# A fused two-block network on one core: the rotary embedding's partition-block transfers issued from SyncE's queue instead of ScalarE's

## The reference, cut to what matters

```python
def rope(x):
    half = HEAD_DIM // 2
    ...
    x1 = x[..., :half].astype(jnp.float32)
    x2 = x[..., half:].astype(jnp.float32)
    out = jnp.concatenate([x1 * cos - x2 * sin, x2 * cos + x1 * sin], axis=-1)
    return out.astype(x.dtype)
...
    qa = rope(rms_norm(to_heads(a_q, N_HEADS_MOBA), qk_g[0]))
    ka = rope(rms_norm(to_heads(a_k, N_HEADS_MOBA), qk_g[1]))
```

## Time and profile before

| | |
|---|---|
| median of 3 runs | 2808.93 us (2806.44 to 2811.38) |
| profiled execution | 2807.05 us |
| its span (first to last instruction) | 2805.2 us |
| PE busy | 2519.4 us (90%) |
| DVE busy | 1328.8 us (47%) |
| POOL busy | 1128.6 us (40%) |
| ACT busy | 1075.1 us (38%) |
| DMA issues `raw<-in_stream`, SPq | 206 of 1024 KB |
| DMA issues `hraw<-xs`, ACTq | 96 of 64 KB |

### The profile page before, as it was taken

One profiled execution on the slowest core, in us unless ns is written; L12 is line 12 of the kernel. 1 busy time (PEld: TensorE's weight loads), 2 busy tenths in 40 slices (PEclk: granted clock), 3 DMA queues, 4 the chain that ended last, 5 costly groups with the idle time before them and its releaser, 6 DMA issues.

```text
span 2805.2 us, 31247 instructions
## 1 busy us (share of the span) xinstructions
PE 2519.4 (90%) x11290; PEld 2022.4 (72%) x11290; DVE 1328.8 (47%) x2101; ACT 1075.1 (38%) x1530; POOL 1128.6 (40%) x828
## 2 busy tenths in 40 slices
PE   6999999679999999999997799999988687896867
PEld 5887887457887888887875578878866565765656
DVE  5454034654444034440255544540676666566663
ACT  4333233534332143331334443331454442464542
POOL 3554445214455445554453044544532222422222
PEclk9999999789999999999998799999999898998989
DMA  3222223102222222222232022222321211211111
GB/s 146 99 91 104 90 104 106 60 16 90 101 93 90 93 102 91 91 103 90 104 105 75 1 90 105 90 105 90 135 68 46 68 46 46 99 52 67 47 66 60
DMA packets 37470, 233.25 MB, mean 83 GB/s; under 512 B 5632, under 2 KB 5632, under 8 KB 10624
## 3 DMA queue, kind: packets, MB, share of 16 engines
q1 hardware_dynamic: 30816, 218.12, 21.8%
q10 hardware_dynamic: 6560, 13.84, 1.7%
HBM read 223.55 MB, written 2.10 MB: 80 GB/s over the span
## 4 chain that ended last, share of the span: by engine, by line
issue 62%; POOL 37%; POOLq 1%
POOL w_lo L412 37%; POOLq L406 0%; POOLq L410 0%; POOLq L202 0%; POOLq L412 0%; POOLq L1776 0%
## 5 line engine op out<-in xcount | busy, mean ns | idle before, releaser
L412 POOL TENSOR_TENSOR w_lo<-raw,w_hi 128x512 fp32r<-128x512 f32 x824 | 1128.4, 1401 | 1676.0 <-ACT w_hi L854 1675.7
L420 PE MATMUL ps<-h_hi,w_hi 128*128 128x512 f32 x2304 | 928.3, 403 | 32.3 <-DVE h_lo L1234 10.7
L421 PE MATMUL ps<-h_lo,w_hi 128*128 128x512 f32 x2304 | 907.7, 394 | 0.0
L422 PE MATMUL ps<-h_hi,w_lo 128*128 128x512 f32 x2304 | 906.2, 393 | 0.0
L854 ACT ACTIVATE w_hi<-raw 128x1024 fp32r<-128x1024 f32 x412 | 413.2, 1051 | 841.2 <-PE ps L422 833.1
L420 PEld LDWEIGHTS ps<-h_hi,w_hi 128*128 128x128 f32 x2304 | 439.8, 191 | 132.7 <-issue 18.8
L421 PEld LDWEIGHTS ps<-h_lo,w_hi 128*128 128x128 f32 x2304 | 439.8, 191 | 93.5 <-issue 5.3
L422 PEld LDWEIGHTS ps<-h_hi,w_lo 128*128 128x128 f32 x2304 | 439.1, 191 | 94.2
L420 PE MATMUL ps<-hid_hi,w_hi 128*128 128x512 f32 x704 | 280.8, 399 | 7.5 <-DVE hid_lo L1228 7.5
L421 PE MATMUL ps<-hid_lo,w_hi 128*128 128x512 f32 x704 | 277.9, 395 | 0.0
L422 PE MATMUL ps<-hid_hi,w_lo 128*128 128x512 f32 x704 | 277.9, 395 | 0.0
(11 more groups left out here) (264 smaller groups left out, 2595.5 us busy)
## 6 DMA issues: line engine op xcount, KB each, us to landing
raw<-in_stream SPq DMA_DIRECT2D x206, 1024.0 KB, 4.8
hraw<-xs ACTq DMA_DIRECT2D x96, 64.0 KB, 2.0
x_sb<-in_x ACTq DMA_DIRECT2D x1, 2048.0 KB, 11.0
out_x<-x_sb SPq DMA_DIRECT2D x8, 256.0 KB, 2.7
mem_sb<-in_mem ACTq DMA_DIRECT2D x1, 1024.0 KB, 13.7
rec_sb<-in_recip ACTq DMA_DIRECT2D x2, 512.0 KB, 4.2
memn<-in_mem ACTq DMA_DIRECT2D x1, 1024.0 KB, 4.9
dist_sb<-in_dist ACTq DMA_DIRECT2D x2, 448.0 KB, 3.2
```

The source lines that it names most:

```text
L412: ins = gp.tensor_tensor(w_lo[:, s, c], raw[:, s, c], w_hi[:, s, c].bitcast(F32), ALU.subtract)
L420: pe.matmul(dst, l_hi, r_hi, start=first, stop=False)
L421: pe.matmul(dst, l_hi, r_lo, start=False, stop=False)
L422: return pe.matmul(dst, l_lo, r_hi, start=False, stop=last)
```

## The change

The four DMAs of each turn are issued by SP, in the stream that loads the panels, and no longer by ACT. ACT's `turn` keeps its two activations and loses its two waits and four DMA issues. SP's rolled loop ends with the first block's panels and the next two; the panels from `BASE2 + 2` on are loaded by a written-out sequence, and behind the load of panel 2 gi + 3 of a layer stand the two turns of group gi, gi = 2 to 7. There SP waits for `xs_ready` and for `hn_rot`.

```diff
-            with sp.Fori(1, (ALL_PANELS + SPARE_PANELS) // 2) as i:
+            with sp.Fori(1, BASE2 // 2 + 1) as i:
                 for s in range(2):
                     sp.wait_ge(lo_split, 2 * i + s - 1)
                     sp.dma_start(raw[:, bass.ds(s, 1), :],
                                  stream[bass.ds(2 * i + s, 1)].rearrange("a p n -> p a n")
                                  ).then_inc(raw_ready[s], 16)
+
+            def turn(l, gi, j):
+
+                rot = 12 * l + 2 * (gi - 2) + j
+                sp.wait_ge(xs_ready, rot + 1)
+                if rot:
+                    sp.wait_ge(hn_rot, rot)
+                for i in range(4):
+                    o, n = 32 * i, 32 * (i ^ 1)
+                    sp.dma_start(hraw[o:o + 32, 1, :], xs[n:n + 32, j, :]).then_inc(turned, 16)
+
+            for p in range(BASE2 + 2, ALL_PANELS + SPARE_PANELS):
+                sp.wait_ge(lo_split, p - 1)
+                sp.dma_start(raw[:, p % 2, :], stream[p]).then_inc(raw_ready[p % 2], 16)
+                l, at = divmod(p - BASE2, LAYER2_PANELS)
+                if at % 2 and 2 <= (at - 3) // 2 < GROUPS and l < LAYERS:
+                    for j in range(2):
+                        turn(l, (at - 3) // 2, j)
...
-                rot0 = 12 * l + 2 * (gi - 2)
-
                 def turn(j):
 
                     g = v2_all[:, bass.ds(NV2 * l + G_QK + 2 * gi + j, 1)]
                     act.activation(xs[:, j, :], ps[:, 4 + 2 * j, :], ACT.Copy, scale=g).then_inc(xs_ready, 1)
                     act.activation(sq[:, j, :], ps[:, 4 + 2 * j, :], ACT.Square).then_inc(hn_in, 1)
-                    act.wait_ge(xs_ready, rot0 + j + 1)
-                    if j == 1:
-                        act.wait_ge(hn_rot, rot0 + 1)
-                    for i in range(4):
-                        o, n = 32 * i, 32 * (i ^ 1)
-                        act.dma_start(hraw[o:o + 32, 1, :], xs[n:n + 32, j, :]).then_inc(turned, 16)
```

## The result

The changed kernel takes 2788.83 us (median of 4 runs, 2785.12 to 2790.46), beside 2810.03 us for the kernel before (4 runs, 2806.44 to 2811.38). The ratio is 0.9923, with a 95% interval of 0.9911 to 0.9935: 21.2 us less. The profiled execution's span went from 2805.2 to 2783.2 us, PE's busy time stayed (2519.4 and 2520.6 us), and so did the mean granted clock (0.949 and 0.951).

A forecast was written before the change was run, and what follows sets the result against it. The chain from ACT's `turn(1)` issues to `qk_lo` sets the ordinary stage's end: 17.7 us there plus 3.2 in memory stages, 20.9 off 2807.05, 2786.1 profiled, 2788.0 as median; range 2778 to 2799 us.

The forecast's parts named there:

- What bounds the kernel: Ordinary stages end with PE waiting 10.5 us for `qk_lo`, its only listed wait there; `turn(1)`'s issues are on that chain.
- turn(0) in ordinary stages: Step 2, ten times: ACT is free 2.1 us sooner, but PE multiplies without pause and hides it; counted as nothing.
- turn(1): Step 4 of ten ordinary stages: `vp_hi` starts 1.57 us sooner, limited by PE's transposes of v, and DVE's chain follows.
- GpSimd, 0.2 us each: Ordinary stages: POOL's second split moves less than DVE, freeing `L1223` and overlapping `qk_lo`; DVE ends 0 to 0.3 us sooner.
- Clock: An 8.7 us wait still drops PE to 1.2 GHz and the restart stays as slow; counted as nothing.
- Memory stages: Two stages: PE's waits for ACT's exponentials up to step 5 vanish, 3.2 us; bounds nothing to 9.8 us.
- Added to SP: SP issues four DMAs per turn at 612 ns; blocks land 2.6 us before DVE needs them, so no cost.
- The price named for a panel in flight: In SP's ring, blocks behind a panel would be late by up to 4.8 us; no panel was seen in flight.
- GpSimd takes part of it back: Rival, 0.12: POOL's earlier split meets and stretches DVE's `L1519` in ordinary stages; gain only 9 to 12 us, about 2798.
- Nothing shows: Rival, 0.07: at `vp_hi` ACT's freed time is swapped for a wait on PE's transposes of v; 2807 to 2809 us.
- The blocks come late: Rival, 0.06: slow SP issues or queueing behind a panel make DVE wait for `turned`; say +6 us, about 2815.
- The signs: Expected in the trace: ten `qk_lo` waits of 8.5 to 9.0 us, no early exponential waits in memory stages, no DVE wait for blocks.

The follow-up runs named there:

- late_split: Changed kernel with the second panel's split moved from step 7 to behind the exponentials of the next stage's step 0: 2745.36 us, ratio 0.9767 to the kernel before.
- split_behind_v: Changed kernel with ACT's 2 us split of the first panel moved behind `vp_hi`: 2794.15 us, ratio 0.9953 to the kernel before.
- eight_extra_issues: Changed kernel with eight more half-size DMAs of constants issued by SP ahead of k's four: 2792.19 us, ratio 0.9936 to the kernel before.
- late_split_turns_first: `late_split` with SP issuing q's turn ahead of the panel load: 2744.36 us, ratio 0.9761 to the kernel before.
- act_still_issues: Changed kernel with ACT also issuing four DMAs per turn, of constants into an unused tile: 2818.94 us, ratio 1.003 to the kernel before.

## Why the prediction was right

**What bounds the kernel.** The chain from ACT's issues over `vp_hi` to `qk_lo` was read rightly. With k's turn alone the gain is 17.8 us; with ACT kept busy it is gone. One reading was too broad: the wait for `qk_lo` is not PE's only one in every such stage. In the stage behind each memory stage PE also waits 2.3 us for `att`, and in the second ordinary stage of layer 0 1.26 us for `ms` (L1557). The first stayed with the change, the second went.

**turn(0) in ordinary stages, costed at nothing.** Their total in the two runs with q's turn alone is 0.02 and 0.7 us above that of before, so PE covers it as said. Those runs are 4.6 to 5.8 us faster all the same, of which 0.4 to 0.9 us is seen in the memory stages. The term was not wrong where it stood, but some gain of q's turn was missed, and its place is open.

**turn(1), 1.57 us each.** `vp_hi` moved by 1.59 us and starts right behind PE's transposes, the limit that the prediction named. The exponential starts 0.04 us after `nmx`, as said.

**GpSimd, 0.2 us each, bound 0.3.** PE's wait shrank by 1.91 us in the stages with 10.50, of which `vp_hi` explains 1.59; 0.32 is left for the overlap. It came about as described: `L1233` runs free, `qk_lo` is stretched. The size was just past the bound.

**Clock, counted as nothing.** This is the term that was mis-sized. The waits shrank by 19.1 us, and the stages by 16.15: the rest of the stages became 2.9 us longer over ten, although the 1.26 us wait for `ms` went, so some 4.2 us are to be explained. The windows show how the clock came in, here in one stage of each kernel. First a stretch of the changed kernel in the wait and two after the restart at 2271.76:

```profile
2266.00:2268.00 2.00, 0.00 (x0) 0.00 (x0) 1.93 (x3) 0.51 (x1) 2.00 (x2) 0.58 0.00 0
...
2274.00:2276.00 2.00, 2.00 (x8) 1.71 (x7) 0.16 (x2) 1.18 (x2) 0.00 (x0) 0.50 0.34 143
2276.00:2278.00 2.00, 2.00 (x9) 1.63 (x8) 1.08 (x1) 1.99 (x5) 0.00 (x0) 0.86 0.00 0
```

Then the kernel before, whose stage starts at 2281.62:

```profile
2284.00:2286.00 2.00, 2.00 (x9) 1.73 (x9) 0.28 (x1) 1.32 (x2) 0.00 (x0) 0.73 0.00 0
```

In this pair PE's clock was back at the upper level (2.4 GHz) 3.5 us after the restart before the change, and 4.8 us after it (0.86 in 2276 to 2278, so from about 2276.6). The pair alone is no rule, for the return varies from stage to stage. Another stage of the kernel before, restarted at 2630.17 behind the same 10.50 us wait, got it back only after 6.5 us:

```profile
2636.00:2638.00 2.00, 2.00 (x9) 1.65 (x8) 0.65 (x3) 0.43 (x3) 0.00 (x0) 0.84 0.02 4
```

Over the eight ordinary stages that start behind such a wait, the return took 3.5 to 6.5 us before (mean 4.5) and 4.8 to 6.7 after (mean 5.5). The two that start behind a memory stage restart at the upper level; there the clock falls inside the stage and stays low for 3.4 us before and 6.8 after. In all, PE had the lower level (1.2 GHz) for 43 us outside the ten waits before and for 57 after. A microsecond of it costs about half a microsecond where PE has no other wait: the stages of the kernel before take 35.2 us without their wait at 3.5 us of low clock and 36.6 at 6.5. At that rate the longer low stretches cost some 5 us (an estimate, without the part of them that falls into the wait for `att`), near the 4.2 that are missing. "The restart stays as slow" was the step that failed, by 0.3 us per stage, net of the wait for `ms` that went. With the 0.14 us by which the waits shrank more than forecast, that makes 1.62 us per stage instead of 1.77, and 16.15 in ten instead of 17.7. The shorter wait of `late_split` is no remedy: it too restarts at 0.50, for 5.0 to 6.0 us. Why the return comes sooner or later is not settled, nor that the shorter wait delays it; no run varied it by itself.

**Memory stages, 3.2 us.** 3.9 measured (2.29 and 1.64). The five waits went from 3.20 to 0.54 us; a later wait for `pt_lo` is 0.2 us shorter in each layer (1.11 before), and layer 0 had the lower clock for 1.1 us less.

**Added to SP, nothing.** Right: 591 ns per issue (612 taken), landing in 2.0 us, DVE held once for 0.2 us; four issues more cost nothing. The price named for a panel in flight, a turn late by up to 4.8 us, was too high: issued 0.43 us behind a panel, as close as it came in `late_split`, the blocks landed in 4.5 to 4.7 us (median), 2.5 to 2.7 late. It was no argument between the two engines either, for behind a panel ACT's blocks landed as late as SP's (3.1 us each, 1.7 us behind the panel's issue).

**The sum.** Forecast 20.9 us off 2807.05. The profiled span fell by 22.0: 16.15 + 3.93 in the stages and 1.9 elsewhere, which the prediction did not have and which is no more than runs differ by. That 20.9 comes so close to the 22.0 of the profiled executions and the 21.2 of the medians is luck in part: the clock took 4.2 us that were not counted, and 1.4 us more from the waits, 1.3 from the wait for `ms`, 0.7 from the memory stages and the 1.9 elsewhere made up for it.

**The rivals.** *GpSimd takes part of it back:* no; `L1529` of step 4 ends at 2252.32 and POOL begins at 2252.32, so they stay apart. `split_behind_v` shows what it costs when POOL and the chain do stand worse: about 5 us. *Nothing shows:* refuted by `vp_hi`, which starts 1.59 us sooner, and by the 17.8 us of k's turn alone. *The blocks come late:* they don't, and the price put on it was too high. The prediction added a late landing to the stage in full. `eight_extra_issues` held DVE for 2.3 us in each ordinary stage and cost 3.4 us in all against the changed kernel's 2788.83 (4.8 in the traces' ten stages), because the instructions held back came out from under POOL.

**The signs.** Most came as named. Two of the ten waits were 9.08 and 9.05 us, just above the 8.5 to 9.0 given, each memory stage kept a wait of 0.27 us for an exponential, and DVE once waited 0.2 us for the blocks.

## What to carry to other kernels

A DMA issue is work of the engine that issues it, though busy time does not count it: four issues of 0.6 us stood ahead of a chain that another engine waited for, and on an engine without such a chain they cost nothing. Look for idle time put down to "issue", follow it to whoever waits last, and count only the issues that lie in the part of the stage which that chain sets.

When two engines slow each other down, an edit moves both, and its worth depends on which instructions come to lie beside each other: a 2.3 us delay in a stage cost 0.3 to 0.5 us of it, and moving a split out of the head of the chain gave 5 us in one kernel and cost 5 in the other. The largest gain here (43.5 us on top of the change's 21.2) came from asking what ran beside the remaining chain, and moving that to where PE sets the pace: `late_split_turns_first`, at 2744.36 us, beats both kernels.

## What was not expected of the hardware

- Four DMA issues on ACT mostly took 2.71 us while SP issued four at the same time (`act_still_issues`), and 2.44 us alone.
- A 64 KB transfer issued 1.7 us behind a 1 MB panel landed in 3.1 us from SP's ring and in 3.1 us from ACT's, and in 2.0 us with nothing in flight.
- DVE's stretch beside POOL differs by instruction: 1.23 to 2.12 us for a 128x1024 subtraction, 0.69 to 1.60 for a cast, 1.29 to 3.27 for two multiplications of 128x512; POOL's own four parts take 5.04 to 6.81 us. An instruction that reads PSUM was not stretched (0.68).
- Behind the same wait of 10.5 to 11.0 us PE's clock came back 3.5 to 6.5 us after the restart; behind 8.6 to 9.1 us it took 4.8 to 6.7.
